# More couples by Strassen's seven products in a four-part feed-forward chain, with two of four weight sums added up by DMA

## The reference, cut to what matters

```
def swiglu(x, w_gate, w_up, w_down):
    return (jax.nn.silu(x @ w_gate) * (x @ w_up)) @ w_down
...
for l in range(DEPTH_2):                       # 2
    x = x + 0.5 * swiglu(rms_norm(x, norm_ffn1[l]), ...)
    x = x + hybrid_mixer(rms_norm(x, norm_mix[l]), ...)
    x = x + 0.5 * swiglu(rms_norm(x, norm_ffn2[l]), ...)
return rms_norm(x, norm_final)
```

## Time and profile before

| | us |
|---|---|
| three runs | 2606.81, 2607.59, 2609.87 (median 2607.59) |
| the profiled execution | 2607.42 |
| its span, first to last instruction | 2605.6 |
| PE busy | 2505.1 (96%) |
| DVE busy | 1687.8 (65%) |
| ACT busy | 1041.7 (40%) |
| POOL busy | 247.4 (9%) |

### The profile page before, as it was taken

The page is one execution under the profiler, slowest core; times in us unless marked ns, Lnnn a source line. Parts: engine busy times, 40 slices in busy tenths (PEclk is TensorE's granted clock), DMA queues, the critical chain, the costliest instruction groups (busy, mean ns, idle before and its releaser), DMA issues. The chain is left out here.

```text
span 2605.6 us, 36570 instructions
## 1 busy us (share of the span) xinstructions
PE 2505.1 (96%) x14533; PEld 2119.0 (81%) x14533; DVE 1687.8 (65%) x2268; ACT 1041.7 (40%) x1434; POOL 247.4 (9%) x178
## 2 busy tenths in 40 slices
PE   7997997999999999999999989999999999999998
PEld 7876776889897878778898879898887777798896
DVE  5355996668676433668686777777743437677776
ACT  4344884334343224644242443333412255433333
POOL 0002112600002300020000010000050001100000
PEclk9998998999999999999999999999999999999999
DMA  4216994232324321222323233233332213233322
GB/s 145 62 57 209 400 412 168 89 98 98 97 92 134 98 79 52 72 82 96 98 97 97 92 103 98 97 98 98 119 110 84 72 34 97 89 98 98 111 85 81
DMA packets 88896, 292.72 MB, mean 112 GB/s; under 512 B 11522, under 2 KB 16530, under 8 KB 88466
## 3 DMA queue, kind: packets, MB, share of 16 engines
q1 hardware_dynamic: 81634, 264.10, 31.3%
q0 software_dynamic: 6224, 23.60, 2.4%
q10 hardware_dynamic: 864, 2.62, 0.3%
HBM read 276.12 MB, written 12.58 MB: 111 GB/s over the span
## 5 line engine op out<-in xcount | busy, mean ns | idle before, releaser
L507 DVE TENSOR_TENSOR w_lo<-w_raw,w_hi 128x1024 fp32r<-128x1024 f32 (+2 forms) x372 | 455.5, 1225 | 164.3 <-ACT w_hi L502 163.1
L551 PE MATMUL bank_l<-xg_hi,w_hi 128*128 128x512 f32 (+1 forms) x1312 | 515.5, 393 | 18.1 <-DVE w_lo L507 14.5
L502 ACT ACTIVATE w_hi<-w_raw 128x1024 fp32r<-128x1024 f32 (+2 forms) x372 | 370.8, 1005 | 363.9 <-PE bank_l L551 339.4
L551 PE MATMUL bank_l<-xg_lo,w_hi 128*128 128x512 f32 (+1 forms) x1312 | 510.0, 389 | 0.0
L551 PE MATMUL bank_l<-xg_hi,w_lo 128*128 128x512 f32 (+1 forms) x1312 | 507.0, 386 | 0.0
L551 PEld LDWEIGHTS bank_l<-xg_hi,w_hi 128*128 128x128 f32 x1312 | 247.4, 189 | 78.9 <-DVE w_lo L507 14.5
L551 PEld LDWEIGHTS bank_l<-xg_lo,w_hi 128*128 128x128 f32 x1312 | 247.1, 188 | 52.8 <-issue 2.2
L551 PEld LDWEIGHTS bank_l<-xg_hi,w_lo 128*128 128x128 f32 x1312 | 247.6, 189 | 52.1
L551 PE MATMUL bank_l<-hid_hi_ff,w_hi 128*128 128x512 f32 x704 | 279.2, 397 | 1.0 <-DVE worked_ff L2166 1.0
L551 PE MATMUL bank_l<-hid_hi_ff,w_lo 128*128 128x512 f32 x704 | 278.7, 396 | 0.0
L551 PE MATMUL bank_l<-hid_lo_ff,w_hi 128*128 128x512 f32 x704 | 276.6, 393 | 0.0
(11 more groups left out here) (436 smaller groups left out, 4810.6 us busy)
## 6 DMA issues: line engine op xcount, KB each, us to landing
w_raw<-in_ff_gate SPq DMA_DIRECT2D x88, 512.0 KB, 3.7
expert_raw<-in_experts SPq DMA_DIRECT2D x81, 512.0 KB, 18.7
w_raw<-in_in SPq DMA_DIRECT2D x80, 512.0 KB, 3.6
w_raw<-in_ff_down SPq DMA_DIRECT2D x64, 512.0 KB, 3.6
up_raw<-in_ff_up SPq DMA_DIRECT2D x52, 512.0 KB, 4.6
w_raw<-in_ff_up SPq DMA_DIRECT2D x36, 512.0 KB, 3.6
w_raw<-in_out SPq DMA_DIRECT2D x24, 512.0 KB, 3.7
w_raw<-in_ff_down SPq DMA_DIRECT2D x32, 384.0 KB, 3.0
```

The source lines that it names most:

```text
L502: act.activation(split_memory(i)[0], split_part(i), ACT.Copy).then_inc(*panel_hi.done(i))
L507: dve.tensor_tensor(lo, split_part(i), hi.bitcast(F32), ALU.subtract).then_inc(*panel_lo.done(i))
L551: done = pe.matmul(dst, w[:, c * cols:(c + 1) * cols], moving, start=c == 0 and n == 0, stop=c == kc - 1 and n == 2)
```

## The change

`SEVEN` takes every couple from the fourth on (from the ninth in ff1_0): 19 in three stages and 14 in ff1_0, 71 in all. In a group they now stand in a row: 3 to 7, 8 to 15, 16 to 21.

DVE makes only S2 and S4. S1 and S3 are made in `ws_raw`, which has five places now, by DMAs that POOL issues (`weight_sums_pool`): S1 by a plain transfer of A21 and then one that adds A22 in flight (`accum_op=ALU.add`); S3 by ACT writing -A11 (`negate`, a new ACT instruction, 128x512) and a transfer that adds A21 to it. So S3 has the other sign (A21 - A11), and T3 changes its sign with it. Both come straight from HBM; SP loads only the half A22 of an up panel. S1 of couple k+1 is begun while couple k-1 is at work and takes turns in two places; S3 of couple j+1 is begun in couple j, when ACT has come to `negate`.

The quarters of x for T1 to T4 come from ACT (8 copies with scale, 128x512, during couple 0) in all stages but ff1_0, and the making, rounding and rests of T1 to T4 are spread over couples 0, 1 and 2.

The diff, cut to its core:

```
-SEVEN = {... [j for j in (3, 4, 6, 7, 8, 9, 11, 12, 14, 15, 16, 17, 19, 20) ...
+SEVEN = {... [j for j in range(3, sum(FF_GROUPS)) ...
-            up_raw = sb(phase, "up_raw", [P, UP_RAW, PANEL])
-            ws_raw = sb(phase, "ws_raw", [P, 4, PANEL // 2])
+            up_raw = sb(phase, "up_raw", [P, UP_RAW, PANEL // 2])
+            ws_raw = sb(phase, "ws_raw", [P, 5, PANEL // 2])
...
+            def begin(k):
+                j = SEVEN[stage][k]
+                if k >= 2:
+                    pool.wait_ge(*ws_low.upto((stage, SEVEN[stage][k - 2], 1)))
+                    pool.wait_ge(*w_sums.upto((stage, SEVEN[stage][k - 2], "S2")))
+                a21 = panel_source(panel_of[ff_keys(stage, j)[1]])[:, 0:half_w]
+                pool.dma_start(sum_raw(stage, j, "S1"), a21).then_inc(*s1_begun.done((stage, j)))
+            def add(k):
+                ...
+                pool.wait_ge(*s1_begun.upto((stage, j)))
+                pool.dma_start(sum_raw(stage, j, "S1"), a22, accum_op=ALU.add).then_inc(*s1_made.done((stage, j)))
+            begin(0)
+            add(0)
+            for k in range(len(SEVEN[stage])):
+                ...
+                    begin(k + 1)
+                pool.wait_ge(*negated.upto((stage, j)))
+                pool.dma_start(sum_raw(stage, j, "S3"), a21, accum_op=ALU.add).then_inc(*s3_made.done((stage, j)))
+                    add(k + 1)
...
+        def negate(act, stage, j):
+            gate = panel_of[ff_keys(stage, j)[0]]
+            act.wait_ge(*panel_in[slot_of_panel[gate]].upto(gate))
+            past = by_seven_before(stage, j)
+            if past is not None:
+                act.wait_ge(*ws_low.upto((stage, past, 0)))
+            act.activation(sum_raw(stage, j, "S3"), panel_memory(gate)[:, 0:half_w], ACT.Copy, scale=-1.0).then_inc(
+                *negated.done((stage, j)))
...
         def round_sums(act, stage, j, pair):
             ...
             act.wait_ge(*w_sums.upto((stage, j, ("S2", "S4")[pair])))
+            act.wait_ge(*(s1_made if pair else s3_made).upto((stage, j)))
...
         def seven_act(act, stage, g, i, j):
             round_sums(act, stage, j, 1)
             take_first(act, stage, j)
             if not first:
                 silu_act(act, stage, j - 1)
             round_upto(act, up + 1)
+            if more:
+                negate(act, stage, j + 1)
             round_upto(act, up + 2)
             if not first:
                 hidden_act(act, stage, g, i - 1, j - 1)
             if more:
                 round_sums(act, stage, j + 1, 0)
...
         def seven_dve(dve, stage, i, j):
             ...
             if more:
-                for name in ("S1", "S3", "S2"):
-                    sum_of_weights(dve, stage, j + 1, name)
+                sum_of_weights(dve, stage, j + 1, "S2")
```

More of the change, by code:

```diff
@@ L55 @@
 UP_RAW = 2
-SEVEN = {f"ff{f}_{l}": [j for j in (3, 4, 6, 7, 8, 9, 11, 12, 14, 15, 16, 17, 19, 20)
+SEVEN = {f"ff{f}_{l}": [j for j in range(3, sum(FF_GROUPS))
                         if (f, l) != (1, 0) or j >= FF_GROUPS[0]] for f in (1, 2) for l in range(DEPTH_2)}
@@ L429, in split_part @@
         def split_part(i):
[L431 removed]
+            return panel_memory(i)
         def split_memory(i):
@@ L473, in load, with panel_source @@
             engine.dma_start(dst, src).then_inc(loaded[name], 16)
+        def panel_source(i):
+            name, j = order[i]
+            kc, cols = panel_shape(i)
+            at = sum(p[1] * p[3] for p in matrices[name][:j])
+            return dram[name][at:at + P * kc * cols].rearrange("(p w) -> p w", p=P)
         def load_panel(sp, i):
             name, j = order[i]
[L479 to L484, removed]
+            src = dram["experts"][j] if name == "experts" else panel_source(i)
+            if slot_of_panel[i][0] == "up":
+                src = src[:, PANEL // 2:]
             before = before_in_slot[i]
@@ L489, in load_panel @@
                     stage, n, which = by_seven(before)
-                    sp.wait_ge(*w_sums.upto((stage, n, "S3" if which == "up" else "S4")))
+                    if which == "gate":
+                        sp.wait_ge(*w_sums.upto((stage, n, "S4")))
+                        sp.wait_ge(*negated.upto((stage, n)))
             if slot_of_panel[i][0] == "up" and by_seven(i)[1] in SEVEN[by_seven(i)[0]][0:UP_RAW]:
@@ L1816, in build, with sum_raw, raw_of_two, sum_place @@
         gate_value = worked[:, 0:2, :].rearrange("p a t -> p (a t)")
+        def sum_raw(stage, j, name):
+            odd = SEVEN[stage].index(j) % 2
+            return ws_raw[:, {"S3": 0, "S2": 1, "S1": 4 if odd else 2, "S4": 3}[name], :]
+        def raw_of_two(stage, j, pair):
+            odd = SEVEN[stage].index(j) % 2
+            return ws_raw[:, 3:5, :] if pair and odd else ws_raw[:, 2 * pair:2 * pair + 2, :]
+        def sum_place(stage, j, name):
+            odd = SEVEN[stage].index(j) % 2
+            return {"S3": 0, "S2": 1, "S1": 3 if odd else 2, "S4": 2 if odd else 3}[name]
         def x_quarter(part, k, t):
@@ L1852, in sum_weights @@
         def sum_weights(pe, stage, j, name):
-            k = SUMS.index(name)
+            k = sum_place(stage, j, name)
             pe.wait_ge(*ws_low.upto((stage, j, k // 2)))
@@ L2028, in feed_forward_act @@
                     round_ahead(act, ff_down(stage, g, m))
+                    if g < len(FF_GROUPS) - 1 and m == DC - 3:
+                        negate(act, stage, j)
                     if g < len(FF_GROUPS) - 1 and m == DC - 2:
@@ L2037, in rest_of_sums @@
             dve.wait_ge(*ws_high.upto((stage, j, pair)))
-            dve.tensor_tensor(ws_lo[:, both, :], ws_raw[:, both, :], ws_hi[:, both, :].bitcast(F32),
+            dve.tensor_tensor(ws_lo[:, both, :], raw_of_two(stage, j, pair), ws_hi[:, both, :].bitcast(F32),
                               ALU.subtract).then_inc(*ws_low.done((stage, j, pair)))
@@ L2058, in sum_of_weights @@
         def sum_of_weights(dve, stage, j, name):
-            gate, up = (panel_of[k] for k in ff_keys(stage, j))
+            gate = panel_of[ff_keys(stage, j)[0]]
             a11, a12 = panel_memory(gate)[:, 0:half_w], panel_memory(gate)[:, half_w:]
[L2061 to L2065, removed]
             dve.wait_ge(*panel_in[slot_of_panel[gate]].upto(gate))
@@ L2187, in feed_forward_dve @@
                     rest_ahead(dve, key)
-                    if g < len(FF_GROUPS) - 1 and m >= DC - 3:
-                        for name in (("S1", "S3"), ("S2",), ("S4",))[m - DC + 3]:
-                            sum_of_weights(dve, stage, j, name)
+                    if g < len(FF_GROUPS) - 1 and m >= DC - 2:
+                        sum_of_weights(dve, stage, j, ("S2", "S4")[m - DC + 2])
                         if m == DC - 2:
```

73 lines of the change are left out of this document (50 added, 23 removed).

## The result

| | before | after |
|---|---|---|
| median of the runs | 2608.73 us | 2663.15 us |
| lowest and highest | 2606.81 to 2612.27 (4 runs) | 2657.11 to 2665.27 (4 runs) |
| span of the profiled execution | 2605.6 | 2662.0 (the run: 2663.99) |

The changed kernel is slower: its time is 1.0203 of the time before, 95% interval [1.0183, 1.0224]. The forecast was 2591, the range 2568 to 2650; both missed. What came is the rival that the prediction called the turn through S3, and more of it than the 2641 that it gave for T = 4.5. (The turn is the ring of waits by which each couple's S3 hangs on the S4 before it; T is the time from the issue of S3's adding DMA to its landing.)

A forecast was written before the change was run, and what follows sets the result against it. PE, busy 96% of the span, and what makes it wait were taken as the bound. From 2607.4 us, -20.5 (couples), -17.7 and -1.5 (waits) and +23.2 (turn through S3) sum to -16.5: forecast 2591, range 2568 to 2650.

The forecast's parts named there:

- the turn through S3: Rival: in rows of couples by seven this ring becomes the bound, slower from T = 3.96 on; chance 0.30.
- term 3: Rows of couples by seven: turns of 7.1 + T against PE's 10.00 cost +23 us at T = 3.7.
- The upper bound: T of S3's adding transfer: 4.4 us, with 1.4 for 256 KB more by the nearest slope.
- 63T - 210: Loss in us summed over all rows of couples by seven, from T = 3.6 on.
- Term 1: 19 more couples by seven, 1.08 us saved in each: -20.5 us.
- Term 2: Couple 3 in three stages: PE's waits with their clocks, 17.7 us, go; a wait from couple 0 too, -1.5.
- the three waits: PE's waits at couple 3 of three stages for rests of weight sums, 12.6 us in all, were to go.
- the wait of couple 0: PE's wait of 1.53 us, tied to panel rests slowed while POOL adds up quarters, was to go: -1.5.
- the prediction's last sentence: The turn is wrong if PE waits elsewhere than S1 T1 or the couples' period doesn't follow T.
- DVE's own work: DVE's instructions in a couple by seven: 9.3 us, under PE's 10.00, so DVE just fits.
- the near ends: T of S3's transfer: 3.0 us if adding costs nothing extra, 4.4 by the slope; the middle, 3.7, was taken.

The follow-up runs named there:

- r3: The changed kernel with S3's transfer plain instead of adding, so the addition of -A11 is left out; 2607.19 us, ratio to before 0.9990.
- r2: The changed kernel with only POOL's order changed: S3's adding transfer issued ahead of the plain one that begins S1; 2639.78 us.
- r7: The changed kernel with negation and S3's transfer issued first, and negation first also in plain couples ahead of one by seven; 2573.94 us.
- r1: The changed kernel with ACT negating first in a couple by seven and POOL issuing S3's adding transfer ahead of S1's two; 2589.76 us.
- r5: The kernel before with only the new sums of x (quarters by ACT outside ff1_0, rests over couples 1 and 2); 2595.99 us.
- r4: The changed kernel with the old list of 52 couples by seven; 2654.31 us, ratio to before 1.0177.

## Why the prediction was wrong

**The step that failed is the size of T in term 3.** The prediction took 3.7, the middle of 3.0 and 4.4, and called 3.96 the point where the sign turns. It measured 4.4: 1.1 for the adding (r3), 0.45 for the plain transfer just ahead on POOL's queue (r2), and 2.9, as much as L1979's plain transfer, for the rest. The upper bound, from the slope of 0.7 per 128 KB, had been the right value by luck: its 1.4 stood for the adding alone, which costs 1.1. The prediction did name the second cause, the DMA issued just ahead, but as an argument for a rival and without a price; it stood in the order of the instructions for everyone to see.

**The structure of term 3 held.** The turn was put at 7.1 + T; it is 7.32 + T in the changed kernel, in r2 and in r3 (quartiles), at three values of T. The 0.2 are POOL's: it issues 0.29 behind the end of the negation, and I had taken 0.1. Put T = 4.4 and 0.2 more into 63T - 210 and it gives 80. Between the spans of r7 and of the changed kernel lie 88.7 us; the prediction's term left out the three drops of the clock that stayed (waits of 2.87 to 3.15 at couple 3), 1.7 each, 5.1 in all. That makes 85 of 88.7, and the 71 couples by seven, measured one by one, take 85 us more in the changed kernel than in r7.

**What T alone does not explain.** With T = 4.4 alone the prediction would have read 2635, inside its range and still 28 under the result. By the prediction's sum with the runs' numbers the 72 us from 2591 to 2663 are about 44 for T, 13 for the 0.2 in each turn, 5 for the clock at couple 3, 3 for waits there that were longer than priced, 5 for the waits at the ends of stages, for which there was no term, and 1 by which the median of the kernel before rose.

**Term 1 was right.** With the turn out of the way the couples take 9.96 to 10.00 in the long rows (r1, r7), so 1.08 or a little more is saved in each of 19.

**Term 2 was right in place, too large, and not independent of term 3.** It said that the three waits go. By themselves they fall from 12.6 to 4.6 and the clock stays up (r5), worth 13.6 and not 19.2, with the wait of couple 0 gone as said. It said that DVE can begin the gate value when the product is there, and it begins 1.5 later, behind the very rests that had been moved. In the changed kernel S3 of couple 3 hangs on that: it was to be issued 8.2 into couple 2 and went at 10.2. The prediction priced that wait at T - 2.7, which is 1.7 with T = 4.4, and would be 3.7 with the 2.0 of delay; it was 2.98, 2.87 and 3.15. With the negation first in the plain couple (r7) 0.9 is left, near the 1.1 of r5, where no S3 comes by DMA.

**Where PE waits.** The prediction said S1 T1, 0.8 each. In a steady couple PE waits twice, at S2 T2 for pair 0 (0.90) and again at S1 T1 for pair 1 (0.47), since pair 1's rest comes 3.60 behind pair 0's and PE has less work between. Of the 59.1 us 38.2 lie at S2 T2 (45 waits) and 20.9 at S1 T1 (46 waits). By the prediction's last sentence that would speak against the turn; the period, which follows T in three kernels, and r1 speak for it, so it was the place that was read wrong. The other signs came as written: ACT's rounding of pair 0 is released by a DMA, DVE's panel rest in couple 0 takes 1.23, couples 10 to 15 take 7.3 + T.

**DVE's own work, and S1,** were judged right: 9.4 us in a couple, and S1's two transfers (2.9, then 4.8) never kept PE: in the changed kernel pair 1's rounding waits for S4. In r1 ACT does wait for S1's landing at times (0.84 at 1687.27 of its timeline), and the couples still take 9.96.

**The choice behind the number.** Between the near ends, 3.0 and 4.4, the prediction took the middle because the second read is on another side than the first. That reason had no row. The slope of the rows and the transfer issued just ahead, which stands in the order of instructions, both pointed upward.

## What to carry to other kernels

When a stage's time is more than any engine's work in it, look for the ring: follow one instruction to its next occurrence, and add up the links; a transfer inside that ring costs its whole latency in each turn, and the same transfer issued before the ring's slow link cost the couples of the long rows nothing here, even though it took longer (5.5 against 4.4 us). Both the producer and every wait ahead of the issue in the issuing engine's list have to be moved, or little is won (14 and 23 us apart, 73 together). Where an unknown latency sits in a ring, price what stands beside it on the queue, and let no middle value stand without a row; here the upper bound of the rows would have served.

## What the runs showed of the hardware

- A 256 KB transfer from HBM that adds to what is in SBUF takes 1.1 us longer than a plain one in the same place (4.42 and 3.32). Its issue has 0.865 us in the trace instead of 0.54 to 0.57, but does not hold the next one up for so long: in r2 S3's issue starts at 1709.71 and the next at 1710.24, 0.53 later, with 0.89 itself. The latency of adding transfers, 3.5 to 8.2 us over the runs, spreads more than I had thought: in r1 and r7 S3's was 5.5 in the median, issued just as SP's 512 KB gate panel goes out (1676.58 and 1676.82 in r1). That the panel is the reason is not shown.
- Two transfers of POOL issued back to back: the second lands 0.45 us later when a plain one of 256 KB is ahead (r2), and the plain one is delayed from 2.9 to 5.2 when the adding one is ahead.
- A wait costs PE more than the length that the view gives it, at a granted clock of 1.00. In the changed kernel's timeline of PE:

```profile
1356.89 0.38 PE L1869 MATMUL bank_s<-xs_hi,ws_hi 128*128 128x256 f32 x1 [0.90 <-DVE ws_lo L2115]
1357.12 0.28 PE L1869 MATMUL bank_s<-xs_lo,ws_hi 128*128 128x256 f32 x1
1357.23 0.28 PE L1869 MATMUL bank_s<-xs_hi,ws_lo 128*128 128x256 f32 x1
...
1360.50 0.39 PE L1869 MATMUL bank_s<-xs_hi,ws_hi 128*128 128x256 f32 x1 [0.47 <-DVE ws_lo L2115]
```

  The couple takes 11.85: 9.96, the waits of 0.90 and 0.47, and 0.52 besides, 0.26 for each wait. Part of it is how the view counts: a matmul has 0.28 us in it, but the next starts 0.12 behind, so an idle time that is counted from the end of a matmul leaves out 0.16. The rest is the first matmul behind a wait, 0.38 instead of 0.28: the second starts 0.23 later instead of 0.12. The 0.26 are the same in nearly all of the 91 waits, 24 us beside the 59.1 that the view shows. The change in the sum of waits alone would miss a quarter of the loss. PE's busy time takes the 24 us in: for the same list it is 2509.9 in the changed kernel and 2478.1 in r7.
- The clock: behind waits of 2.98, 2.87 and 3.15 us it was granted 0.5, the 1.2 GHz level, for 3.4 us. Behind the steady couples' waits (up to 1.6) and r5's of 1.4 it stayed at 1.00. Between them the length of the one wait does not decide: in r4 the clock fell behind two waits of 1.82 and stayed at 1.00 behind those of 2.20, 2.30 and 2.34 at couple 3.
- ACT's eight copies and POOL's DMA issues beside DVE's rests left these at 1.22 to 1.23 us (80 rests of the changed kernel overlap an issue), where POOL's additions had made one of them 3.36. The Trainium skill (SBUF — State Buffer, "Who interferes with whom") tells both apart in the same way: a GpSimd instruction that reads SBUF contends with a two-input DVE instruction, descriptor generation needs only the write side (the page infers the latter). The trace agrees.
- The Trainium skill (Collectives: The Full Stack, "The bandwidth ceiling: the fold count and why AG ≠ RS ≠ AR") says of the ring's reduce step that its add needs two source reads through one ring, twice the traffic of a copy. The prediction's estimate from it was 0.6 us more for 256 KB. S3's transfer is no such ring step; it took 1.1 more, 0.33 of it in the issue and 0.77 behind it, so the trace agrees in direction and is somewhat above.
